# Down projection in two layouts: 448 tokens as moving columns, 128 tokens as the stationary operand

## The reference, cut to what matters

```python
D_MODEL = 1024
D_FF = 2816
def rms_norm(x, g):
    y = xf * lax.rsqrt(jnp.mean(xf * xf, axis=-1, keepdims=True) + EPS)
    return (y * g).astype(x.dtype)
...
    h = modulate(rms_norm(x, g_pre_ffn), sh2, sc2)
    f = (jax.nn.silu(h @ w_gate) * (h @ w_up)) @ w_down
    x = x + gt2[:, None] * rms_norm(f, g_post_ffn)
```

## Time and profile before

| what | value |
|---|---|
| median of 3 runs | 977.9 us (977.37 to 979.57) |
| the profiled execution's own time | 977.59 us |
| its span | 975.8 us |
| its mean granted TensorE clock | 0.988 |
| PE busy | 926.4 us (95%) |
| DVE, ACT, POOL busy | 60%, 48%, 35% |

### The profile page before, as it was taken

The page is one execution under the profiler, slowest core; times in us unless marked ns, Lnnn a source line. Parts: engine busy times, 40 slices in busy tenths (PEclk is TensorE's granted clock), DMA queues, the critical chain, the costliest instruction groups (busy, mean ns, idle before and its releaser), DMA issues. The chain is left out here.

```text
span 975.8 us, 17662 instructions
## 1 busy us (share of the span) xinstructions
PE 926.4 (95%) x6864; PEld 878.5 (90%) x6864; DVE 582.8 (60%) x1101; ACT 464.3 (48%) x895; POOL 340.0 (35%) x193
## 2 busy tenths in 40 slices
PE   4889999999999999999999899999999999999995
PEld 1688898899998999988888789999999999999995
DVE  4767559897975333153200589999999999200006
ACT  4665334556467554353343584454444547322121
POOL 2031005555363322134444242333333331544450
PEclk9899999999999999999999999999999999999998
DMA  9841013231321013167865401232222322122202
GB/s 363 312 129 49 8 66 98 102 107 69 117 90 68 23 56 139 51 227 267 329 210 185 156 1 44 95 123 87 87 87 88 105 100 90 62 88 89 90 30 97
DMA packets 35619, 111.84 MB, mean 115 GB/s; under 512 B 4240, under 2 KB 9360, under 8 KB 35280
## 3 DMA queue, kind: packets, MB, share of 16 engines
q1 hardware_dynamic: 31152, 102.48, 30.2%
q10 hardware_dynamic: 4112, 6.93, 1.9%
q0 software_dynamic: 272, 1.31, 0.3%
HBM read 100.38 MB, written 10.32 MB: 113 GB/s over the span
## 5 line engine op out<-in xcount | busy, mean ns | idle before, releaser
L1312 POOL TENSOR_TENSOR wlo<-raw,whi 128x1024 fp32r<-128x1024 f32 x53 | 133.0, 2511 | 233.0 <-ACT whi L883 223.7
L1955 PE MATMUL pj<-hh,whi 128*128 128x288 f32 x544 | 124.9, 311 | 5.4 <-ACT zs L964 2.4
L1955 PE MATMUL pj<-hh,wlo 128*128 128x288 f32 x544 | 117.3, 297 | 0.0
L1955 PE MATMUL pj<-hl,whi 128*128 128x288 f32 x544 | 117.2, 297 | 0.0
L1369 POOL TENSOR_TENSOR op_lo<-ssum,op_hi 128x512 fp32r<-128x512 f32 x40 | 53.7, 1365 | 148.6 <-PE pj L2209 131.9
L1955 PEld LDWEIGHTS pj<-hh,whi 128*128 128x128 f32 x544 | 87.4, 192 | 8.2 <-issue 3.8
L1955 PEld LDWEIGHTS pj<-hh,wlo 128*128 128x128 f32 x544 | 88.3, 190 | 0.0
L1955 PEld LDWEIGHTS pj<-hl,whi 128*128 128x128 f32 x544 | 88.2, 190 | 0.0
L1200 ACT ACTIVATE op_hi<-ssum 128x512 fp32r<-128x512 f32 x80 | 50.3, 628 | 72.4 <-DVE ssum L1703 54.4
L1893 DVE RECIPROCAL rstd<-rms 128x288 f32<-128x288 f32 x2 | 3.9, 1954 | 122.3 <-ACT rms L1138 122.3
L1378 POOL TENSOR_TENSOR dlo<-rawd,dhi 128x1408 fp32r<-128x1408 f32 x14 | 46.7, 3333 | 84.4 <-ACT dhi L1260 84.4
(11 more groups left out here) (290 smaller groups left out, 2752.6 us busy)
## 6 DMA issues: line engine op xcount, KB each, us to landing
raw<-in_w_s SPq DMA_DIRECT2D x54, 512.0 KB, 4.4
sraw<-in_w_s SPq DMA_DIRECT2D x40, 512.0 KB, 4.2
rawa<-in_w_ada SPq DMA_DIRECT2D x32, 512.0 KB, 6.2
rawd<-in_w_d SPq DMA_DIRECT2D x16, 704.0 KB, 4.0
raw<-in_w_ada SPq DMA_DIRECT2D x16, 512.0 KB, 10.3
g_raw<-gz ACTq DMA_DIRECT2D x16, 288.0 KB, 2.2
gate<-g_raw SPq DMA_DIRECT2D x8, 576.0 KB, 3.8
rawv<-in_w_v SPq DMA_DIRECT2D x8, 324.0 KB, 5.0
```

Source lines behind the costliest of these rows:

```text
L1312: pool.tensor_tensor(rest, raw_of(c), whole.bitcast(F32), ALU.subtract).then_inc(w_lo, 1)
L1955: ins = mm(pj[tile % 2][:, h, 0:HALF], w[:, slot(c), b:b + P], x[:, kc, h * HALF:(h + 1) * HALF], start=(kc == first and w is whi and x is ...
```

## The change

The columns are cut differently: NA = 448 tokens stay as they are (features on partitions) and fit in one PSUM bank, and the last NT = 128 tokens are computed with tokens on partitions.

- **448 columns.** The down loop has 22 x 3 = 66 matmuls of 448 columns for each of the 8 output tiles. All 8 tiles run in the same loop; the split of tile 7 in two halves is gone.
- **128 tokens, 22 steps.** Step j takes the chunk j of f: the stationary operand is `fh[j]` or `fl[j]`, columns 448 to 575, and the moving one is a row block of w_down, 128 x 1024, in its parts `wt_hi` and `wt_lo`. Two banks (`lg`) of 512 columns each take the sum over all 22 steps: 6 matmuls of 512 columns for a step.
- **Where.** Ten steps run after blocks 2, 3, 4, 5, 6, 8, 9, 10, 12 and 13 of the 16 blocks, and twelve after the last block.
- **A second copy of w_down** (22 loads of 512 KB, `wt_raw`) in another order of columns. ACT makes wt_hi, DVE wt_lo; POOL makes wt_lo for steps 15, 17, 19 and 21. There are three buffers for the early steps and six for the late ones; a buffer is loaded again when the step that had it is done. Buffer 5 (step 15) is free only after the last block.
- **x1 of the 128 tokens** is transposed by 8 TensorE transposes after tile 1, and copied back by ACT. The gain row goes by a store and a broadcast load (`g_row`, `gT`) to all partitions.
- **End.** stat3 runs once for 448 columns after step 10. The reciprocal is written to PSUM (`pvb`), and DVE mixes the four pairs' products (`scaled_y`) and sums (`residual`) with its rests for the steps. After the last step: two squares with a row sum (ACT), a sum, root and reciprocal of one column, the gain row's product, and two fused multiply-adds of 512 columns, each stored.

```diff
+NT = P
+NA = T - NT
...
+STEP_AFTER = (2, 3, 4, 5, 6, 8, 9, 10, 12, 13)
+N_EARLY = len(STEP_AFTER)
+STEP_SLOT = [j % 3 for j in range(N_EARLY)] + [1, 2, 0, 3, 4, 5, 1, 2, 0, 3, 4, 5]
+STEP_POOL = (15, 17, 19, 21)
...
+        def step_free(eng, j):
+            s = STEP_SLOT[j]
+            last = [m for m in range(j) if STEP_SLOT[m] == s]
+            if last:
+                eng.wait_ge(step_used, last[-1] + 1)
+            elif s < 3:
+                eng.wait_ge(st_full, made(N_PAIR - 1, N_PROD - 1))
+                eng.wait_ge(f_ready, FC)
+            else:
+                eng.wait_ge(d_lo, 2 * (KC - 1))
+                if s == 4:
+                    eng.wait_ge(down_used, KC)
+                elif s == 5:
+                    eng.wait_ge(pj_full, full(T_DN + KC - 1))
+        def step_rest(eng, j):
+            s = STEP_SLOT[j]
+            eng.wait_ge(step_hi, j + 1)
+            return eng.tensor_tensor(wt_lo[s][:, :], wt_raw[s][:, :], wt_hi[s][:, :].bitcast(F32), ALU.subtract)
...
@@ SP
+                    for j in range(N_EARLY):
+                        if STEP_AFTER[j] + 1 == 2 * d + k:
+                            load_step(j)
+            for j in range(N_EARLY, FC):
+                load_step(j)
+                if STEP_SLOT[j] == 4 and j < N_EARLY + 6:
+                    sp.wait_ge(xt_out, 3)
+                    sp.dma_start(g_row[0], orms[:, 0:KC]).then_inc(g_row_in, 16)
+                    sp.wait_ge(g_row_in, 16)
+                    sp.dma_start(gT[:, :], g_row.rearrange("o p k -> o (p k)").to_broadcast([P, D])).then_inc(g_row_in, 16)
...
@@ ACT
             for d in range(KC - 1):
-                hi_down(d + 1, 0)
-                hi_down(d + 1, 1)
-                f_tile(T_DN + d, d)
-            for h in range(2):
-                last_tile(T_DN + KC - 1, KC - 1, h)
+                for k in range(2):
+                    hi_down(d + 1, k)
+                    if k:
+                        f_tile(T_DN + d, d)
+                    for j in range(N_EARLY):
+                        if STEP_AFTER[j] + 1 == 2 * d + 2 + k:
+                            step_whole(j)
...
+            for j in range(N_EARLY, N_EARLY + 5):
+                step_whole(j)
+            f_tile(T_DN + KC - 1, KC - 1)
+            act.wait_ge(stat3_full, 1)
+            act.activation(rms3[:, :], tb[:, 0:NA], ACT.Sqrt, bias=eps[:, 0:1], scale=1.0 / D).then_inc(rms3_ready, 1)
+            for j in range(N_EARLY + 5, FC):
+                step_whole(j)
+            for n in range(2):
+                act.wait_ge(tok_full, n + 1)
+                if n:
+                    act.wait_ge(tok_sq, 1)
+                act.activation(junk[:, :], lg[:, n, :], ACT.Square, accum_out=tstat[:, n:n + 1]).then_inc(tok_sq, 1)
+            act.wait_ge(tok_y, 2)
+            act.activation(tstat[:, 3:4], tstat[:, 2:3], ACT.Sqrt, bias=eps[:, 0:1], scale=1.0 / D).then_inc(rms3_ready, 1)
...
@@ POOL
                 squares(1, d, acc2, sq2[d % 3][:, :])
+            for j in STEP_POOL:
+                step_rest(pool, j).then_inc(d_lo, 1)
...
@@ DVE (the loops of the two column halves are removed)
+            for j in range(N_EARLY + 5):
+                low(j)
+            v.wait_ge(rms3_ready, 1)
+            v.wait_ge(xt_out, 2)
+            v.reciprocal(pvb[:, 0:NA], rms3[:, :]).then_inc(rstd_ready, 1)
+            v.wait_ge(rstd_ready, 6)
+            v.wait_ge(pj_act, taken(T_DN + KC - 1, "A"))
+            low(16)
+            scaled_y(0)
+            scaled_y(1)
+            low(18)
+            residual(0)
+            scaled_y(2)
+            residual(1)
+            low(20)
+            scaled_y(3)
+            residual(2)
+            residual(3)
+            v.wait_ge(g_row_in, 32)
+            for n in range(2):
+                v.wait_ge(tok_sq, n + 1)
+                if n:
+                    v.tensor_tensor(tstat[:, 2:3], tstat[:, 0:1], tstat[:, 1:2], ALU.add).then_inc(tok_y, 1)
+                v.tensor_tensor(ytok[:, n * 512:(n + 1) * 512], lg[:, n, :], gT[:, n * 512:(n + 1) * 512], ALU.mult)\
+                 .then_inc(tok_y, 1)
+            v.wait_ge(rms3_ready, 2)
+            v.reciprocal(tstat[:, 4:5], tstat[:, 3:4]).then_inc(rstd_ready, 1)
...
+                v.scalar_tensor_tensor(y, y, tstat[:, 4:5], x, ALU.mult, ALU.add).then_inc(x2_ready, 1)
...
@@ TensorE
+            def step(j):
+                s = STEP_SLOT[j]
+                pe.wait_ge(step_hi, j + 1)
+                wait_step_lo(pe, j)
+                pairs = ((fh, wt_hi), (fh, wt_lo), (fl, wt_hi))
+                order = ([(p_, n) for n in range(2) for p_ in range(3)] if j == FC - 1 else
+                         [(p_, n) for p_ in range(3) for n in range(2)])
+                for p_, n in order:
+                    x, w = pairs[p_]
+                    ins = mm(lg[:, n, :], x[j][:, NA:T], w[s][:, n * 512:(n + 1) * 512], start=(j == 0 and p_ == 0),
+                             stop=(j == FC - 1 and p_ == 2))
...
-            for d in range(KC - 1):
+            for d in range(KC):
...
                         for w, x in ((dhi, fh), (dhi, fl), (dlo, fh)):
-                            for h in range(2):
-                                ins = mm(pj[tile % 2][:, h, 0:HALF], w[k][:, b * P:(b + 1) * P],
-                                         x[kc][:, h * HALF:(h + 1) * HALF],
-                                         start=(kc == 0 and w is dhi and x is fh), stop=(kc == FC - 1 and w is dlo))
+                            ins = mm(pj[tile % 2][:, 0, 0:NA], w[k][:, b * P:(b + 1) * P], x[kc][:, 0:NA],
+                                     start=(kc == 0 and w is dhi and x is fh), stop=(kc == FC - 1 and w is dlo))
                     ins.then_inc(pj_full if k else down_used, 1)
+                    for j in range(N_EARLY):
+                        if STEP_AFTER[j] == 2 * d + k:
+                            if j == 0:
+                                pe.wait_ge(f_ready, FC)
+                            step(j)
+                if d == 1:
+                    for kc in range(KC):
+                        bank = (tb, pvb)[kc // KH]
+                        ins = pe.transpose(bank[:, kc % KH * P:(kc % KH + 1) * P], x1[:, kc, NA:T], ident[:, :])
+                    ins.then_inc(xt_full, 1)
+            for j in range(N_EARLY, FC):
+                step(j)
+                if j == N_EARLY:
+                    pe.wait_ge(xt_out, 2)
+                    stat3()
```

More of the change, by code:

```diff
@@ L635, in wait_down_lo, with step_raw_there, wait_step_lo @@
                 eng.wait_ge(d_lo_vec, k + 1)
+        def step_free(eng, j):
[16 more added lines that the diff above has]
+            return eng.tensor_tensor(wt_lo[s][:, :], wt_raw[s][:, :], wt_hi[s][:, :].bitcast(F32), ALU.subtract)
+        def step_raw_there(eng, j):
+            s = STEP_SLOT[j]
+            eng.wait_ge(raw0_in[s], 16 * (len(range(s, N_ADA0, RAW0)) + STEP_SLOT[:j].count(s) + 1))
+        def wait_step_lo(eng, j):
+            if j in STEP_POOL:
+                eng.wait_ge(d_lo, 2 * (KC - 1) + STEP_POOL.index(j) + 1)
+            else:
+                eng.wait_ge(step_lo, sum(m not in STEP_POOL for m in range(j + 1)))
         def whole(i, k):
@@ L1124, in f_tile, with step_whole @@
                 square_free(d)
[L1125 to L1139, removed]
+                act.activation(sq2[d % 3][:, :], pj[n % 2][:, 0, 0:NA], ACT.Square).then_inc(ysq_ready, 1)
+                for w, c0, c1 in ((1, 0, NS), (0, NS, NA)):
+                    ins = act.activation(ymix[d // 2][:, d % 2, c0:c1], pj[n % 2][:, 0, c0:c1], ACT.Copy,
+                                         scale=gg[:, 1, d, w:w + 1])
+                ins.then_inc(pj_act, 1)
+            def step_whole(j):
+                s = STEP_SLOT[j]
+                step_raw_there(act, j)
+                step_free(act, j)
+                act.activation(wt_hi[s][:, :], wt_raw[s][:, :], ACT.Copy).then_inc(step_hi, 1)
             act.activation(scratch[:, 0:1], eps[:, 0:1], ACT.Sqrt)
@@ L1888, in _, with low @@
             rest_of_f(14, FC)
[L1889 to L1905, removed]
+            def low(j):
+                step_rest(v, j).then_inc(step_lo, 1)
@@ new lines, in scaled_y, with residual @@
+            def scaled_y(i):
+                r2 = pvb[:, 0:NA].unsqueeze(1).to_broadcast([P, 2, NA])
+                v.tensor_tensor(ymix[i][:, :, :], ymix[i][:, :, :], r2, ALU.mult).then_inc(yr3_ready, 1)
+            def residual(i):
+                x2 = x1[:, 2 * i:2 * i + 2, 0:NA]
+                v.wait_ge(yr3_ready, i + 1)
+                v.tensor_tensor(x2, ymix[i][:, :, :], x2, ALU.add).then_inc(x2_ready, 1)
+            for j in range(N_EARLY + 5):
+                low(j)
+            v.wait_ge(rms3_ready, 1)
@@ new lines, in _ @@
+            for n in range(2):
+                v.wait_ge(tok_sq, n + 1)
[5 more added lines that the diff above has]
+            v.reciprocal(tstat[:, 4:5], tstat[:, 3:4]).then_inc(rstd_ready, 1)
```

(1 more changed line is left out.)

100 lines of the change are left out of this document (59 added, 41 removed).

## The result

The changed kernel takes 982.94 us in the median of 6 runs (982.13 to 983.54), the kernel before 979.58 us in 6 (977.37 to 979.98). The ratio as measured is 1.0047, 95% interval 1.0036 to 1.0058. The plain ratio of these two medians is less, 1.0034, and the listed runs don't show why. So 0.3 to 0.5% slower is what can be said. The forecast was 978.4 us, 0.05% over the 977.9 us that the first three runs of the kernel before had given, with a range of 973.6 to 982.0; the time lies above it.

A forecast was written before the change was run, and what follows sets the result against it. TensorE was taken to bound the down projection, with waits on POOL and DVE at its start and in the late stage. 838.9 + 108.6 + 22.6 + 6.4 = 976.5 us of span, forecast 978.4 us, range 973.6 to 982.0.

The forecast's parts named there:

- The sum: Whole span: 838.9 + 108.6 + 22.6 + 6.4 = 976.5 us against 975.8, so +0.7 us.
- The matmul terms: Down projection on TensorE: 203 ns per 448-column matmul, 231 ns per 512-column one; products 137.7 us against 140.6, 2.9 less.
- Tile 0 gives its share back: First tile: matmuls 4.2 us shorter become idle time, since block 2 still waits for POOL's dlo(1, 0) until 838.9.
- The early stage: Block 2 to last block: seven tiles, ten steps and eight transposes take 108.6 us, ending at 947.5.
- The tail: Last main matmul to the end of the span: 6.4 us against 12.2, 5.8 us gained by shorter normalisation.
- The step that fills the late stage: After the last block: DVE and POOL operations with two SBUF inputs take turns; 22.6 us, 4.5 of them waits.
- the order in the late stage: After the last block: POOL's rest 19 waits for DVE's rest and residual 0, ending at 16.6; last step ends at 22.6.
- the second possibility: Late stage: waiting POOL gets its turn after each DVE operation, rest 20 comes behind rest 21, last step to 24.0.
- The rival of the clock: Late stage: waits of 1 to 2 us bring the 1.2 GHz level; four steps cost 5.6 us more, 984; chance 0.04.
- Late steps fed in time: Late stage: DVE and POOL overlap with little loss, last step at 19.2; time 975.0, down to 973.3; chance 0.27.
- loads land late: Late stage: weight loads landing at 6.5 us instead of 4.1 add 3.8 us, 982.2; chance 0.15.
- Early waits: Early steps: three waits of 0.2 to 0.5 us, priced with POOL's turn before rest 20: +2.4, 980.8; joint chance 0.14.

The follow-up runs named there:

- Holding the order: Changed kernel with POOL's rest 19 waiting for residual 0 and its rest 21 for DVE's rest 20; 1.0022 times the kernel before.
- filling the wait: Changed kernel with 15 extra matmuls of 448 columns on TensorE after step 19, into an unused bank; 1.0037 times the kernel before.
- both fillers: Changed kernel with 15 extra matmuls after step 19 and 10 more between tile 0 and block 2; 1.0030 times the kernel before.

## Why the prediction was wrong

**Right, and shown.** The sum had +0.7 us on the span; from tile 0 on, which is all that the sum is about, the profile has +4.7. Of the 4.0 us between them 3.8 lie in the late stage.
- The matmul terms: 203.6 ns for 448 columns (203 taken), 1.39 to 1.40 us for a step (1.39). The Trainium skill's rule (TensorE: Matmul & The Clock Gate, "Wait — 56ns, not 53.3ns?"), N / 2.4 GHz and 2.5 ns, gives 189.2; these rows speak against it as the ones of before did.
- Tile 0 gives its share back: 18.19 us from its first matmul to block 2, against 18.23 before, with a wait of 2.25 us (2.5 forecast). Moving dlo(1, 0) to DVE brought 1.5 us of it.
- The early stage: 109.0 us against 108.6, no waits at steps. Of the 0.4, about 0.25 is block 2, and most of the rest the 0.6 ns for each of the 462 matmuls.
- The tail: 6.2 against 6.4.
- The step that fills the late stage: POOL's and DVE's two-input operations exclude each other. With the products in PSUM the residuals ran unhindered.

**The step that failed: the order in the late stage, and the clock behind it.** The prediction wrote: "POOL waits for DVE's rest and residual 0", from one row in which POOL waited through several DVE operations. In the changed kernel POOL's rest 19 got the port between rest 18 and residual 0, and rest 21 got it when DVE went on to product 2, which doesn't need it. This order stood in the text as the second possibility, with the last step at 24.0 instead of 22.6; it was priced as 1.4 us and left to a rival. The Trainium skill (SBUF — State Buffer, "SBUF: two separate sides") says that whichever of the two starts first holds the shared ports for the whole instruction and the other fully blocks. The trace agrees with the blocking (3.28 us for 1.08). Which one is next when both wait is a step beyond that sentence, and the prediction took it from there as a turn after each operation. In this late stage the two did take turns. Beside tile 0 of the same profile they didn't: POOL's dlo(1, 0), from 835.01, took 4.76 us for 3.22, ending 3.05 us after the last of DVE's fl (836.72), so more than one fl went ahead of it. What decides it stays open.

What was not seen is that both rivals are one. With this order TensorE's wait before step 20 is 3.6 us, the granted clock falls to the 1.2 GHz level, and steps 20 and 21 take 2.7 us more. The rival of the clock had a chance of 0.04, since waits of 1 to 2 us had left the clock alone in the earlier trace rows; it was never weighed against the longer wait that the other order gives. Added up: order 1.1 (step 20 began at 20.94 us, so at the pace of the other steps step 21 would have ended at 23.7, near the 24.0 of the rival), clock 2.7, together the 3.8 us that the late stage is longer. Holding the order gave the forecast's 22.8 us, and filling the wait gave back 2.2 with the order as it was.

**A smaller miss.** A 2.25 us wait before block 2 was costed as itself. Block 2 takes 1.5 us more when the clock falls behind it, in four of the nine profiles with that wait (the two of the changed kernel without an edit are not among the four). The forecast had taken the 1.94 us wait at 818.7 as evidence of no fall. That was one execution, and the slices it cited are too coarse: in the profile of the changed kernel the stretch from 820 to 830 us has a clock of 0.83, and its slice of the page still reads 9.

**Rivals.** "Late steps fed in time" didn't come true. The load on the changed kernel's chain took 4.5 us (3.9 to 5.5 in the profiles of the edits), and its waits are put down to rests, so "loads land late" is not what happened. Early waits: none. The order and the clock came true together: 1.1 us for the 1.4 priced, and two slow steps, 2.7 us, for the four, 5.6 us, of the rival of the clock.

## What to carry to other kernels

Price a wait of TensorE by its length and by what runs behind it: waits of 2.2 us here were followed by a low clock in four of nine profiles, and of 3.6 us in both that had one, at which the next work costs up to double. Where DVE and POOL both have operations with two SBUF inputs, work out the queue in both orders, since small shifts of when a load lands turned it here: POOL's rest 19 went ahead of residual 0 where its operand was ready 0.6 us before DVE's rest 18 ended, and behind it where it was ready 0.2 us after (the profile with both fillers). Putting one operand of an operation in PSUM, or all of the operations on one engine, took the question away for them. And ask of a tile made shorter whether anything that it waits for got earlier: here the first tile's 4.2 us were idle time, and moving one operation of 3.2 us to the free engine returned 1.5 of them.

## What the runs showed of the hardware

- A POOL operation can slip in between two DVE operations that follow on each other, both with two SBUF inputs (rest 19, between rest 18 and residual 0), or when DVE goes on to one with an input in PSUM (rest 21); the next DVE operation with two SBUF inputs then waits for it (3.28 and 2.25 us for 1.08). Beside tile 0 POOL waited through more than one of DVE's instead.
- After waits of 2.2 to 2.4 us TensorE's granted clock fell in some executions and not in others (block 2 at 6.95 or 8.3 to 8.5 us; step 20 after 2.4 us at full pace); after 3.6 us of waiting it fell in both profiles of the changed kernel, and 15 matmuls without use in the wait kept it at 1.00.
- Also around tile 0 the stretch from 820 to 830 us showed a clock of 0.83 in eight of the twelve profiles of the changed kernel and its edits, after the wait of 1.9 us ahead of it, where before showed 1.00. It cost nothing there: in profiles without it TensorE only waited longer for DVE's fl (1.0 us in all).
